# Two narrow projections of a 256-token block on one core: the narrow matrix moves from the stationary to the streamed side

## What is computed

```python
u = rmsnorm(h, mix_norm) @ w_in_mix          # 2048 x 4112: 8 blocks of 512 columns and 16 more
gate_lr = u[..., 4096:]                      # the 16 columns
log_alpha = log_sigmoid(gate_lr @ w_alpha + b_alpha) / 16

proj = x @ w_in_a                            # 2048 x 6224
iq, ik, iw = proj[..., 5120:6144], proj[..., 6144:6208], proj[..., 6208:6224]
# ik (64 columns, rotated by position) and iw (16) are the 80 columns of the narrow stage
```

## Time and profile before

| | |
|---|---|
| median of 3 runs | 2741.19 us |
| profiled execution, its own time | 2739.0 us |
| its span | 2737.3 us |
| PE, busy share of the span | 99%, 12254 matmuls |
| PEld (weight loads) | 81% |
| DVE, ACT, POOL | 57%, 47%, 2% |
| mean DMA rate | 198 GB/s |
| granted TensorE clock in the profile's 40 slices | 9 (90% or more) in each |

### The profile page before, as it was taken

One profiled execution on the slowest core, in us unless ns is written; L12 is line 12 of the kernel. 1 busy time (PEld: TensorE's weight loads), 2 busy tenths in 40 slices (PEclk: granted clock), 3 DMA queues, 4 the chain that ended last, 5 costly groups with the idle time before them and its releaser, 6 DMA issues.

```text
span 2737.3 us, 34409 instructions
## 1 busy us (share of the span) xinstructions
PE 2712.9 (99%) x12254; PEld 2227.3 (81%) x12254; DVE 1550.2 (57%) x1904; ACT 1295.7 (47%) x1697; POOL 57.6 (2%) x66
## 2 busy tenths in 40 slices
PE   9999999999999999999999999999999999999999
PEld 7888888888888788888888888877888888777877
DVE  6555555555735466555555555757555576555566
ACT  6443444344544445443444344545544554554453
POOL 0000000000000000000000000030000000120000
PEclk9999999999999999999999999999999999999999
DMA  9876677676745476765676666754455576445654
GB/s 313 249 207 195 209 217 207 193 215 182 257 140 177 147 230 215 222 210 192 208 216 209 194 213 187 258 171 154 151 192 182 171 223 208 154 139 196 187 176 138
DMA packets 414584, 540.63 MB, mean 198 GB/s; under 512 B 40080, under 2 KB 262544, under 8 KB 413680
## 3 DMA queue, kind: packets, MB, share of 16 engines
q1 hardware_dynamic: 412800, 530.46, 62.1%
q0 software_dynamic: 1504, 8.34, 0.8%
q10 hardware_dynamic: 144, 0.04, 0.0%
HBM read 520.34 MB, written 18.35 MB: 197 GB/s over the span
## 4 chain that ended last, share of the span: by engine, by line
PE 93%; DVE 2%; DMA 1%; ACT 1%; POOL 1%; SPq 1%; issue 1%; ACTq 0%; POOLq 0%; DVEq 0%
PE bank L1325 29%; PE bank L1327 29%; PE bank L1326 29%; DVE wlo L1666 1%; PE bank L1284 1%; DMA raw<-in_ffn_w_in_dram 1%; SPq L1206 1%; POOL rope_b L884 1%; ACT whi L1412 1%; PE bank L1031 0%; DMA hidden_squares<-hidq 0%; PE bank L832 0%; PE bank L816 0%; PE bank L1048 0%; PE bank L1057 0%
## 5 line engine op out<-in xcount | busy, mean ns | idle before, releaser
L1666 DVE TENSOR_TENSOR wlo<-raw,whi 128x1024 fp32r<-128x1024 f32 (+2 forms) x975 | 1150.0, 1186 | 1112.5 <-ACT whi L1412 1107.4
L1412 ACT CAST whi<-raw 128x1024 fp32r<-128x1024 f32 (+2 forms) x975 | 986.1, 1016 | 1304.5 <-PE bank L1327 1297.8
L1325 PE MATMUL bank<-whi,p_hi 128*128 128x512 f32 x2016 | 794.6, 394 | 4.5 <-DVE wlo L1666 3.2
L1327 PE MATMUL bank<-whi,p_lo 128*128 128x512 f32 x2016 | 785.0, 389 | 0.0
L1326 PE MATMUL bank<-wlo,p_hi 128*128 128x512 f32 x2016 | 784.7, 389 | 0.0
L1325 PE MATMUL bank<-whi,q_hi 128*128 128x512 f32 x1696 | 665.2, 392 | 2.8 <-DVE wlo L1666 2.8
L1327 PE MATMUL bank<-whi,q_lo 128*128 128x512 f32 x1696 | 660.4, 389 | 0.0
L1326 PE MATMUL bank<-wlo,q_hi 128*128 128x512 f32 x1696 | 660.0, 389 | 0.0
L1325 PEld LDWEIGHTS bank<-whi,p_hi 128*128 128x128 f32 x2016 | 378.4, 188 | 91.2 <-issue 13.2
L1326 PEld LDWEIGHTS bank<-wlo,p_hi 128*128 128x128 f32 x2016 | 378.6, 188 | 80.1 <-issue 3.1
L1327 PEld LDWEIGHTS bank<-whi,p_lo 128*128 128x128 f32 x2016 | 378.4, 188 | 79.7
(11 more groups left out here) (274 smaller groups left out, 1009.5 us busy)
## 6 DMA issues: line engine op xcount, KB each, us to landing
raw<-in_ffn_w_in_dram SPq DMA_DIRECT2D x704, 256.0 KB, 3.0
raw<-in_ffn_w_out_dram SPq DMA_DIRECT2D x320, 256.0 KB, 3.1
raw<-in_w_in_a_dram SPq DMA_DIRECT2D x192, 256.0 KB, 3.1
raw<-in_w_in_mix_dram SPq DMA_DIRECT2D x128, 256.0 KB, 3.2
raw<-in_w_ple_gate_dram SPq DMA_DIRECT2D x128, 256.0 KB, 3.9
raw<-in_w_in_b_dram SPq DMA_DIRECT2D x128, 256.0 KB, 3.1
raw<-in_w_out_mix_dram SPq DMA_DIRECT2D x64, 256.0 KB, 3.5
raw<-in_w_o_a_dram SPq DMA_DIRECT2D x64, 256.0 KB, 3.4
```

Of the source, the lines that this page charges most:

```text
L1325: pe.matmul(o, xht, wh, start=(kt == t_first), stop=False)
L1327: ins = pe.matmul(o, xlt, wh, start=False, stop=(kt == t_last))
L1412: act.copy(whi[:, c % SPLIT, 0:n, 0:w], raw[:, c, 0:n, 0:w]).then_inc(hi_done, 1)
L1666: dve.tensor_tensor(wlo[:, c % SPLIT, 0:n, 0:w], raw[:, c, 0:n, 0:w], whi[:, c % SPLIT, 0:n, 0:w].bitcast(F32), ALU.subtract).then_inc(lo_ ...
```

## The change

Both narrow stages are computed like the wide ones: the special case in `multiply` goes, so that the 128 x 128 tiles of x are stationary and 16 or 80 columns of the weight stream, in both token halves. ACT evacuates each half with one activation, times `rstd`, straight into `rtm` or `index_tail`. `narrow_back` and `narrow_normed` go, with their two places in the bank plan, and those that waited for the place "tail" wait for the evacuation (`acc_free`).

```diff
-            for name, m in (("sum0", 0), ("rB", 2), ("sum1", 1), ("y0", 2), ...
+            for name, m in (("sum0", 0), ("sum1", 1), ("y0", 2), ...
...
-            plan("tail", 3)
...
-        def narrow_back(pe, src, w, name):
-
-            b = use(name)
-            for t in range(TT):
-                ins = pe.transpose(b[:, t * w:(t + 1) * w], src[0:w, t * P:(t + 1) * P], ident[0:w, 0:w])
-            filled(ins, name)
-
-        def narrow_normed(act, dst, w, name):
-
-            b = take(act, name)
-            for t in range(TT):
-                ins = act.activation(dst[:, t, :], b[:, t * w:(t + 1) * w], ACT.Copy, scale=rstd[:, t:t + 1])
-            release(ins, name)
...
                 pe.wait_ge(acc_free, by_name["mix_decay"].a0 + 1 + FREE0)
                 pool_sums(0)
-                narrow_back(pe, ab["rt"], 16, "rB")
...
-                wait_freed(pe, "rB")
...
-            if step == ("mix_qk", 0, 0):
-                narrow_normed(act, ab["rtm"], 16, "rB")
...
-            if step == ("a_kv", 0, 0):
-                pe.wait_ge(acc_free, by_name["a_tail"].a0 + 1 + FREE0)
-                narrow_back(pe, ikt, 80, "tail")
...
-            if step == ("a_kv", 0, 0):
-                narrow_normed(act, ae["index_tail"], 80, "tail")
...
-            wait_freed(pool, "tail")
+            pool.wait_ge(acc_free, by_name["a_tail"].a0 + 1 + FREE0)
...
-                wait_freed(dve, "tail")
+                dve.wait_ge(acc_free, by_name["a_tail"].a0 + 1 + FREE0)
...
-                        if s.kind == "narrow":
-
-                            if t:
-                                continue
-                            o = dst[0][0:s.width, 0:SEQ]
-                            pe.matmul(o, wh, xh[:, kt, :], start=(kt == t_first), stop=False)
-                            pe.matmul(o, wl, xh[:, kt, :], start=False, stop=False)
-                            ins = pe.matmul(o, wh, xl[:, kt, :], start=False, stop=(kt == t_last))
-                            continue
                         xht, xlt = xh[:, kt, t * P:(t + 1) * P], xl[:, kt, t * P:(t + 1) * P]
                         pe.matmul(o, xht, wh, start=(kt == t_first), stop=False)
...
-                    w = s.width
-                    act.copy((ab["rt"] if s.name == "mix_decay" else ae["ikt"])[0:w, :], pair[0][0:w, 0:SEQ]).then_inc(acc_free, 1)
+                    dst = ab["rtm"] if s.name == "mix_decay" else ae["index_tail"]
+                    for t in range(TT):
+                        ins = act.activation(dst[:, t, :], pair[t][:, 0:s.width], ACT.Copy, scale=rstd[:, t:t + 1])
+                    ins.then_inc(acc_free, 1)
```

More of the change, by code:

```diff
@@ L365, in build @@
         if "mix_qk" in by_name:
-            for name, m in (("sum0", 0), ("rB", 2), ("sum1", 1), ("y0", 2), ("sum2", 0), ("y1", 3), ("sum3", 1), ("y2", 2), ("y3", 3),
+            for name, m in (("sum0", 0), ("sum1", 1), ("y0", 2), ("sum2", 0), ("y1", 3), ("sum3", 1), ("y2", 2), ("y3", 3),
                             ("rT", 0), ("z0", 0), ("z1", 1), ("b0", 0), ("suf0", 2), ("b1", 1), ("suf1", 3),
```

## The result

The changed kernel takes 2763.06 us, the median of 4 runs (2761.44 to 2769.05), against 2740.92 for the kernel before in the same comparison: +22.1 us, a ratio of 1.0084 (95% interval 1.0066 to 1.0101). The forecast was slower, by +7.8 us, with a range up to 2763.0. The sign was right and the size was not: the time lies at the very end of the range, beyond it by 0.06 us, and nearly three times the forecast loss.

A forecast was written before the change was run, and what follows sets the result against it. PE was taken to bound the kernel, carrying 93% of the chain. 4.47 + 4.56 - 0.42 - 0.19 - 0.61 = +7.8 us gave 2749.0 us, range 2746.5 to 2763.

The forecast's parts named there:

- The streams, at full clock: Both narrow stages: 96 load-set steps of 0.112 us each, +4.47 us for 16 columns and +4.56 us for 80.
- fp32r steps might be longer (0.120): Upper end for the narrow stages' step, 0.120 us, as fp32r steps carry a little more than plain ones; a guess.
- the price of nothing: 80-column stage: the 80 streamed columns stay hidden beside the load and add nothing to the step.
- the plain fp32 rate: Rival, 80-column stage: columns stream at the plain fp32 price, 139 ns for 80, +2.6 us, 2751.6 us; chance 0.12.
- two records a matmul: Rival, both narrow stages: few-column matmuls issued as two records with a load each, 21.5 us more, 2770.5 us; chance 0.04.
- a load took less than 0.11 us: Rival, both narrow stages: loads go quicker, at 0.060 us a step the sum is -2.2 us, 2739.0 us; chance 0.07.
- Transposes and waits: Transposes back gone after the narrow stages, -0.42 us (mix) and -0.19 us (a_kv); wait for index keys gone, -0.61 us.
- The wait for `wlo`: First wide matmul after a narrow stage: PE's 0.44 us wait goes, already counted in the 16-column stage's +4.47 us.
- that for the index keys: Line 766, PE waiting for POOL's `ikd`: the keys come in time after the change, -0.61 us.
- line 562's place: PE's wait a wide chunk after the narrow stage: ACT is in time with 0.8 us cover, so no cost.
- The clock: Rival: clock falls with few columns streaming; half the 16-column stage gives +7.4 us, 2756.4 us, all +13.4, 2762.4; chance 0.27.
- the forecast's case for both stages: Clock rival's case of the fall coming in both narrow stages: priced only as "more" than 2762.4 us.

The follow-up runs named there:

- the kernel with 128 columns: Changed kernel, but both narrow stages stream 128 columns of the weight slots, the further results unread: 2747.70 us, 1.0028 against the kernel before.
- 256 columns: Changed kernel, but both narrow stages stream 256 columns of the weight slots, the further results unread: 2749.96 us, 1.0036 against the kernel before.
- each stage alone: Two kernels, against the kernel before: only the 16-column stage by tokens, 2754.30 us (1.0049); only the 80-column stage, 2752.64 us (1.0045).
- packed: Changed kernel with low weight part beside the high one, 64 matmuls and loads a stage, DVE evacuating: 2741.82 us, 1.0006 against the kernel before.
- in turns: Changed kernel, but even chunks of the narrow stages stream 256 columns, odd ones 16 or 80: 2751.03 us, 1.0037 against the kernel before.
- the last version: Low weight part beside the high one, with DVE's evacuation moved ahead of the next stage's fourth-chunk split: 2742.81 us, 1.0008 against the kernel before.

## Why the prediction was wrong

- **The streams, at full clock: right.** 0.1115 to 0.112 us a step, set by the 128 x 128 load, from one burst in the trace of before; the kernel with 128 columns, at full clock, gives +7.3 us for the whole of the forecast's +7.8, and its trace meets the sum stretch by stretch. That fp32r steps might be longer (0.120) showed only with 256 columns.
- **80 columns: the price of nothing was right**, the plain fp32 rate wrong: 80, 16 and 128 columns have one step. No two records a matmul either, and no stage in which a load took less than 0.11 us on average.
- **Transposes and waits: right.** The wait for `wlo` and that for the index keys are gone, -0.6 us for the latter as worked out. PE never waited at line 562's place.
- **The clock: this step failed.** The forecast took the level of before, full, for the stretch after, and gave 0.27 to its fall. The runs showed 0.50 for 13.9 and 10.4 us of the two stages and for 3.2 and 3.3 us of wide matmuls behind them, 8.1 and 6.4 us that the sum had at nothing. The rows gave no reason for that: no stretch of before streamed 7 ns of 112, and I set against the rival that "loads run without a pause, and 80 columns stream more". The changed kernel's trace shows that loads without a pause do not hold the clock, and its second stage that 80 columns do not either; the runs with more columns show that the loads do not lower it. The rival's own price for one stage (+7.4 us) was close to each stage's (8.1 and 6.4); it had 48 slow steps and 9 wide ones, where 64 and 47 slow steps and 8 wide ones came. It came twice, and the forecast's case for both stages had only "more". The range's end of 2763 was meant for the fall in one stage; that two stages came out 0.06 us beyond it is chance.
- **Two slips that change nothing.** The range's lower end of 2746.5 adds its +7.0 to the profiled execution's 2739.0 and not to the median; from the forecast's 2749.0 it would be 2747.7. And of the 4.5 us in the earlier trace rows both waits for `wlo` together are 4.4, not 1.2 to 3.2.

## What to carry to other kernels

When a stage swaps its sides so that few columns stream past a freshly loaded 128 x 128 tile, count its loads and not its columns: here 0.112 us a load whatever is streamed up to 128 columns. Then read the granted clock through the stretch and behind it, and not the mean of a long slice: in this kernel it halved in both stages, at 16 and at 80 columns, and the wide matmuls behind them paid as well. If the form is wanted, stream columns that nobody reads: with 128 it cost +7.3 us where the bare version cost +22.1; or put both parts of a split weight beside each other, which brought it to within 1.4 to 2.8 us of the kernel before by the traces, and no better than it.

## What the runs showed of the hardware that I had not expected

- PE and PEld 100% busy by the profile's rows, and the granted clock still at 0.50: 13.90 of 13.90 us. The busy share does not tell what the clock will be.
- Streaming more was faster: 128 columns 2747.7 us, 16 and 80 columns 2763.1 us, on the same loads. Between 80 and 128 columns nothing was tried.
- Short stretches at 0.50 (some 3.4 us each) come and go between executions of one kernel, at places where PE has done transposes and waited: at 2069 and 2530 us in the changed kernel, at 2514 us in the one with 128 columns (last row there), none in the profiled execution of before. The other traces have one that starts between 2510 and 2521 us (each stage alone, 256 columns, packed), two (in turns) or none (the last version). The timed runs of the kernel before seem to have them too: of 12 in one comparison, 10 had a mean granted clock of 0.999 (2739.7 to 2742.6 us) and the two with 1.000 took 2738.5 and 2740.4 us; one such stretch makes 1 - 0.5 x 3.4 / 2740 = 0.9994. Each costs about 1.5 us, so part of the spread of all these medians is theirs, and the profiled execution of before, 2739.0 us, was one without. The windows of the changed kernel and then of the one before, around the same place:

```profile
2526.60:2530.00 3.40, 1.42 (x10) 1.20 (x11) 2.54 (x4) 1.75 (x5) 0.00 (x0) 1.00 0.67 202
...
2530.00:2533.40 3.40, 3.40 (x10) 2.63 (x9) 1.19 (x2) 0.46 (x1) 0.00 (x0) 0.50 0.24 87
```

```profile
2503.30:2506.70 3.40, 1.22 (x11) 0.81 (x9) 2.42 (x3) 1.77 (x4) 0.00 (x0) 1.00 0.64 193
...
2506.70:2510.00 3.30, 3.30 (x18) 2.75 (x17) 1.29 (x2) 1.05 (x3) 0.00 (x0) 1.00 0.34 119
```

PE was busy for 1.42 of 3.40 us ahead of the fall, and in the kernel before for 1.22 of 3.40 us with no fall behind it; its one wait there is 2.18 us long in both. What decides when they come stays open.
